# Last pair of the second attention: the projection's copies behind the next step's probabilities and the high and low parts

## The reference

```python
s = jnp.einsum('bhqd,bhkd->bhqk', qi, k).astype(jnp.float32) * scale
s = s + cqi[..., None] - c[:, :, None, :]
s = jnp.where(kpos[None, :] <= qpos[:, None], s, -jnp.inf)
pr = jax.nn.softmax(s, axis=-1)
return jnp.einsum('bhqk,bhkd->bhqd', pr.astype(v.dtype), v)
...
gate = jax.nn.sigmoid(x @ ple_w_gate[i] + ple_b_gate[i])
x = x + gate * (p[i] @ ple_w_proj[i])
```

## Time and profile before

| what | us |
|---|---|
| median of 3 runs | 2450.26 (2449.76 to 2451.69) |
| the profiled execution | 2450.21 |
| its span, first to last instruction | 2448.5 |
| PE busy | 2414.1 (99%) |
| DVE busy | 1579.5 (65%) |
| ACT busy | 1097.2 (45%) |
| POOL busy | 1368.4 (56%) |

### The profile page before, as it was taken

The page is one execution under the profiler, slowest core; times in us unless marked ns, Lnnn a source line. Parts: engine busy times, 40 slices in busy tenths (PEclk is TensorE's granted clock), DMA queues, the critical chain, the costliest instruction groups (busy, mean ns, idle before and its releaser), DMA issues. The chain is left out here.

```text
span 2448.5 us, 35802 instructions
## 1 busy us (share of the span) xinstructions
PE 2414.1 (99%) x11528; PEld 1995.1 (81%) x11528; DVE 1579.5 (65%) x2284; ACT 1097.2 (45%) x2027; POOL 1368.4 (56%) x1221
## 2 busy tenths in 40 slices
PE   8999999999999999999999999999999999999999
PEld 6788888888788878888888888777888888888887
DVE  8855552344677786435666666656868777777885
ACT  5433333301666661126777777832432333344441
POOL 5698887534455564443222222254289888666683
PEclk9999999999999999999999999999999999999999
DMA  4122223579200014432111111441133333487652
GB/s 144 61 82 64 69 69 112 183 265 325 94 31 26 30 32 167 138 120 71 61 61 60 60 57 60 145 134 53 53 114 124 109 120 114 146 276 220 190 182 84
DMA packets 128949, 275.65 MB, mean 113 GB/s; under 512 B 14144, under 2 KB 14528, under 8 KB 128848
## 3 DMA queue, kind: packets, MB, share of 16 engines
q1 hardware_dynamic: 84800, 157.85, 20.7%
q10 hardware_dynamic: 44048, 116.58, 13.3%
HBM read 206.41 MB, written 67.96 MB: 112 GB/s over the span
## 5 line engine op out<-in xcount | busy, mean ns | idle before, releaser
L688 POOL TENSOR_SCALAR whi<-raw 128x512 fp32r<-128x512 f32 x190 | 134.4, 707 | 339.2 <-PE bank L906 171.3
L690 POOL TENSOR_TENSOR wlo<-raw,whi 128x512 fp32r<-128x512 f32 x190 | 267.2, 1406 | 15.9
L703 POOL TENSOR_TENSOR wlo<-a,whi 128x512 fp32r<-128x512 f32 x114 | 163.9, 1438 | 43.6 <-ACT whi L1890 43.4
L906 PE MATMUL bank<-b_lo,whi 128*128 128x512 f32 x448 | 175.3, 391 | 0.0
L906 PE MATMUL bank<-a_hi,whi 128*128 128x512 f32 x416 | 164.9, 396 | 5.5 <-DVE a_lo L2797 3.8
L969 PE MATMUL bank<-b_hi,whi 128*128 128x512 f32 x384 | 156.9, 408 | 0.2 <-ACT f_raw L1677 0.2
L969 PE MATMUL bank<-b_hi,wlo 128*128 128x512 f32 x384 | 150.7, 392 | 0.0
L969 PE MATMUL bank<-b_lo,whi 128*128 128x512 f32 x384 | 150.1, 391 | 0.0
L814 POOL COPY fc<-fc 128x128 f32<-128x128 f32 x96 | 28.0, 292 | 193.0 <-DVE mx L2727 193.0
L1890 ACT ACTIVATE whi<-a 128x512 fp32r<-128x512 f32 x114 | 70.7, 628 | 131.9 <-PE bank L1246 50.2
L906 PE MATMUL bank<-b_hi,whi 128*128 128x512 f32 x320 | 125.4, 392 | 1.0 <-ACT up_g L2282 0.6
(11 more groups left out here) (791 smaller groups left out, 7857.0 us busy)
## 6 DMA issues: line engine op xcount, KB each, us to landing
raw<-in_w SPq DMA_DIRECT2D x202, 256.0 KB, 2.6
a<-in_pairs SPq DMA_DIRECT2D x152, 256.0 KB, 2.7
fc<-c_scr ACTq DMA_DIRECT2D x32, 512.0 KB, 3.6
wd_scr<-wd SPq DMA_DIRECT2D x55, 256.0 KB, 5.2
wd<-in_down SPq DMA_DIRECT2D x44, 256.0 KB, 4.5
xs_scr<-made ACTq DMA_DIRECT2D x40, 256.0 KB, 2.7
h_scr<-up_y ACTq DMA_DIRECT2D x13, 512.0 KB, 2.6
raw<-wd_scr SPq DMA_DIRECT2D x26, 256.0 KB, 2.9
```

The costliest lines, as they stand in the source:

```text
L688: nc.gpsimd.tensor_scalar(hi, src, 1.0, 1.0, ALU.mult, ALU.mult).then_inc(w_hi, 1)
L690: nc.gpsimd.tensor_tensor(lo, src, hi.bitcast(F32), ALU.subtract).then_inc(w_lo, 1)
L703: nc.gpsimd.tensor_tensor(ring[1][pos], src[:].rearrange("p (k c) -> p k c", c=P), ring[0][pos].bitcast(F32), ALU.subtract).then_inc(ww_lo, 1)
L906: last = nc.tensor.matmul(psum_ap, ws[w][:, k, :], a[:, kt, hs(h)], start=(first and i == 0 and j == 0), stop=(final and i == n - 1 and j ...
```

## The change

In the loop over the steps of forget_pair, the call of ple_out(s - 1) is moved on two engines. On ACT it stood ahead of normalise(s + 1) and high(n); now it stands behind both. On DVE it stood between maxima(s + 2) and low(n); now it stands behind low(n). At step 6 (s == NB - 2) DVE's copy stays ahead of maxima, as before. Nothing is added or removed.

```diff
--- before.py
+++ after.py
@@ -1760,12 +1760,12 @@
                 for s in range(NST):
                     if fills and s in LEAVES and s < NST - 2:
                         forget_out(*following, LEAVES[s])
-                    if not fills and s:
-                        ple_out(s - 1)
                     if s + 1 < NST and s != NST - 2 and (fills or s > 0):
                         normalise(s + 1)
                     for n in CHUNKS_OF[s]:
                         high(n)
+                    if not fills and s:
+                        ple_out(s - 1)
                     if s == NST - 3 and isinstance(it, int) and it * 2 + pp == NPAIR - 2:
                         p_load(0)
                         p_load(1)
@@ -2765,10 +2765,10 @@
                         maxima(s + 2)
                     if s == 0:
                         v_lo(fx, fv, flips[1][:], 1, it * 4 + (2 * pp + 1))
+                    for n in CHUNKS_OF[s]:
+                        low(n)
                     if not fills and s and s != NB - 2:
                         ple_out(s - 1)
-                    for n in CHUNKS_OF[s]:
-                        low(n)
                     if s > 1 and s % 4 == 1:
                         add(s - 2)
                     if fills and s == NST - 3:
```

## The result

The changed kernel took 2462.64 us (median of 6 runs, 2459.46 to 2463.07) against 2450.44 for the kernel before on the same chip: a ratio of 1.0045, 95% interval 1.0036 to 1.0055. It is slower by 12.2 us. The forecast was 2460.4, with a range of 2456 to 2465.5.

The account below looks back on a forecast made before the run. TensorE, busy 99%, was taken as the bound. Later copies lengthen the stage from 55.39 to 65.2 us (+9.8); with 0.35 at the end, +10.2 on 2450.21 gives 2460.4, range 2456 to 2465.5.

Parts of the forecast that it names:

- The sum: Projection stage of forget_pair's last call: step times add to 65.2 us against 55.39, 9.8 longer.
- parts 1 and 2: ScalarE's copy at odd steps: chain 2.04 us at step 5; VectorE's at even steps but 6: 2.46 at step 4.
- signs that were named: Right if stage about 65 us, parts wait 1.1 to 2.7 (even), 0.5 to 1.5 (odd), transposes at one step only.
- Step 10: Step 10 of the stage: 4.43 us, including 0.22 of normalise(11) in the way.
- Step 6: Step 6 of the stage, VectorE's copy still ahead of maxima: 3.82 us, with no wait left.
- The 0.35 added for the last forget_hi and forget_lo: Next stage's first product needs both, which follow the last part: 0.35 us more beyond the stage.
- What moves besides: Work queued behind the copies moves with the stage, none late; POOL's mask row follows maxima: nothing charged.
- The credit for low parts: TensorE's waits for low parts in the stage, 4.3 us, credited as gone, all but those of step 7.
- A: Rival: long gaps bring the clock down, at step 14 or up to three times, 1.5 us each: 2462 to 2465; chance 0.15.
- B: Rival: only VectorE's move costs, even steps add 3.9 us, the end takes back 0.35: 2453.7; chance 0.07.
- C: Rival: faster, all 7.5 us of TensorE's waits go: 2442.7, or 2445.9 without the copies' 3.2; chance 0.02.
- D: Rival: no effect, as the copies would wait for the same events anyway: 2450 us; chance 0.03.

Follow-up runs that it names:

- e4: Against the kernel before, VectorE's copies ahead of maxima at steps 2, 4, 6, 10, 12, copy 13 ahead of inverse: 2449.22 us, ratio 0.9994.
- e1: ScalarE's move alone (copy behind normalise and high parts), against the kernel before: 2454.37 us, ratio 1.0012.
- e2: VectorE's move alone (copy behind low parts, step 6 exempt), against the kernel before: 2461.32 us, ratio 1.0044.
- e8: The changed kernel again, unaltered, for another profile: one execution of 2462.41 us, stage 67.01 us.
- e6: Against the kernel before, VectorE's copies ahead of maxima at 2, 6, 10, copy 13 ending step 13, three forget_lo one step later: 2450.25 us, ratio 0.9997.
- e9: Against the kernel before, ScalarE's copy between normalise and high; VectorE's ahead of maxima at 2, 6, 10, copy 13 ending step 13: 2449.73 us.
- e10: e9 with ScalarE's copy ahead of normalise at steps 5 and 13: 2450.21 us, ratio 0.9997 to the kernel before.

## Why the prediction was right

**The sum.** 65.2 was forecast for the stage, 65.67 measured, and fifteen of the sixteen steps came within 0.1. The chains of parts 1 and 2 are in the timelines as they were priced: from the end of the values to part 4, 1575.39 to 1577.86, 2.47 us for 2.46; from the first transpose to part 5, 1579.32 to 1581.37, 2.05 for 2.04; at step 14, 1617.43 (0.12 after the start of the last value product, as the ones before it are spaced) to 1620.16, 2.73 for 2.74. So rows of the kernel before carried the durations and the hand-overs between engines, though there they stood in another order. Of the signs that were named, the waits of parts are 0.91 to 2.57 at even steps but 6 and 0.32 to 1.23 at odd ones in the timeline's brackets, their lower ends a little below what was said. Transposes wait for low parts at no step: those of step 7, where a wait was left in the sum, start 0.26 behind the matmul before them, near the pace of 0.23.

**Its mis-sized terms.** Step 10 took 4.68 for 4.43. "0.22 of normalise(11) in the way" was right in kind; but the fold, the exponent and a forget_hi that are queued behind ScalarE's copy of step 9 all moved with it, and the timeline of ACT shows the high part directly behind a later normalise, 0.42 instead of 0.22 behind where the value products (done at 1599.12, and 0.20 for the signal) would have let it start:

```profile
1598.06 1.05 ACT L1698 ACTIVATE b_lo<-f_o 128x1024 fp32r<-128x1024 f32 x1
1599.01 0.71 ACT L1734 ACTIVATE fp<-fp,row_inv 128x512 f32<-128x512 f32 x1
1599.74 0.49 ACT L1742 ACTIVATE fp_hi<-flip 128x384 fp32r<-128x384 f32 x1
```

Step 6 was 0.09 longer, and the end 0.08 shorter. The 0.35 added for the last forget_hi and forget_lo did not come: the last forget_lo ends at 1631.91 (1630.68 and 1.23), and the matmuls that need it start at 1632.06, 0.23 behind the one before, the pace without a wait. The last forget_hi waits for the store of the last part and for the sum of values(15) (add), whichever comes later, here in the timelines of ACT before and after:

```profile
1619.88 1.06 ACT L1698 ACTIVATE b_lo<-f_o 128x1024 fp32r<-128x1024 f32 x1 [1.47 <-DMA ple_scr<-f_raw]
```

```profile
1629.58 1.06 ACT L1698 ACTIVATE b_lo<-f_o 128x1024 fp32r<-128x1024 f32 x1 [1.46 <-DVE f_o L2748]
```

Before, the store came last, 3.7 behind the end of the last copy (1616.17); in the changed kernel it landed no more than 3.2 behind it (1626.33), and the sum came last. So the later part cost nothing: forget_hi starts 2.32 behind the start of the next stage, and before 2.34. The next stage's work on the tiles ahead of the last covers that, with nothing to spare; before, the matmul in this place waited 0.11.

**What moves besides.** "None is late" held for TensorE in the changed kernel, but for step 10. ScalarE's normalise did wait for inverse, 2.9 us in all for 0.2 before, where TensorE did not need it yet. How near the bound is, e4 shows: there maxima(9) came early, and the mask row on POOL took long enough, for the row not to be ready, which the prediction had listed as moving along at no cost. The credit for low parts was right, and e1 and e2 show whose it is: ScalarE's later copies.

**The rivals.** A is not another outcome than the forecast but one that lies on top of it in some executions, at step 14 as written: +1.35 in one profile of four. That profile (e8) shows a sign that the prediction had named as showing it wrong, a granted clock below 1.00 in the stage. The profiled execution came 0.9 below the forecast: 0.5 more in the stage, 0.35 that did not come, and 1.1 less outside it; that the first two cancel in part is luck. The median lies 2.2 above the forecast, among the 2462 to 2465 of A, as it falls into the upper group of executions. A fall of the clock at step 14 gives 1.35 of such a difference where it is seen; what gives the rest the runs leave open. B fell by e1 (ScalarE alone costs at least 2.6). Its price for VectorE's move, 3.5, was far too small as well: e2's stage is 8.12 longer, as the even steps of the forecast already held the credit for low parts that comes only with ScalarE's move. C fell by the result itself; and by e4 to e6, e9 and e10 at most 1.2 of its 7.5 us was to be had, and not by going behind the low parts. D fell by the stage.

## What to carry to other kernels

An instruction that is moved behind others in an engine's queue takes over all their waits: ask what the passed ones wait for, and whether whoever waits for the moved one has work until then. Here to pass normalise, whose input was ready, cost nothing net; to pass high and low parts, which wait for products of the same step, cost 0.5 to 1.4 us at all steps but one, though the accumulator had long been full. In e4, e6 and e9 most of the waits taken away at one step came up again at a later one, so count whole stages, not steps.

## What the runs showed of the hardware

The same wait of 2.56 to 2.57 us before part 14 was followed by a granted clock of 1.00 in three profiles of the changed kernel and in that of e2, and of 0.50 in one (e8). In e1 the clock was at 0.50 after a wait of 2.05, where the slow pace began not with the first matmul behind the wait but 0.82 later (1608.81 to 1609.63). In these runs a wait of this size was a risk, not a fixed price: about 1.4 to 1.6 us when it struck.

In e4 the second mask row on POOL took 1.67 us where the first took 0.63. It started at 1583.61, 0.03 behind VectorE's forget_lo of 1.21 (1583.58), which reads two operands from SBUF, and ended 0.49 behind its end. The Trainium skill (SBUF — State Buffer, section "SBUF: two separate sides") says that a VectorE instruction with two SBUF inputs and a GpSimd one that reads SBUF exclude each other, the later one being held until the first is done. The trace agrees. In the changed kernel it shows twice in a row behind the stage, in the timelines of DVE and POOL, the first time with VectorE as the later one:

```profile
1626.66 2.17 DVE L2696 TENSOR_TENSOR a_hi<-f_o,b_lo 128x1024 fp32r<-128x1024 f32 x1 [0.33 <-ACT b_lo L1698]
```

```profile
1626.46 1.29 POOL L690 TENSOR_TENSOR wlo<-raw,whi 128x512 fp32r<-128x512 f32 x1
1627.72 1.59 POOL L688 TENSOR_SCALAR whi<-raw 128x512 fp32r<-128x512 f32 x1
```

forget_lo took 2.17 for 1.21, having started 0.20 behind POOL's first instruction, and ended 1.08 behind its end. POOL's second took 1.59 where the five in the stage take 0.62 or 0.63, and ended 0.48 behind the end of forget_lo. No run here tries it by itself.
